# The token Fourier transform of a hybrid trunk on sums and differences of mirrored tokens, with half of the frequencies

## The reference, cut to what matters

```python
def _fourier(f, w_f):
    B, L, _ = f.shape
    fg = f.reshape(B, L, FNET_GROUPS, FNET_GROUP_DIM).astype(jnp.float32)
    z = jnp.fft.fft2(fg, axes=(1, 3), norm='ortho').real.astype(f.dtype)
    return z.reshape(B, L, FNET_DIM) @ w_f
```

## Time and profile before

| | |
|---|---|
| time, median of 3 runs | 1360.46 us (1359.41 to 1366.07) |
| profiled execution, its own time | 1359.2 us |
| its span, first to last instruction | 1357.4 us |
| mean granted TensorE clock | 0.966 |
| TensorE, VectorE, ScalarE, POOL busy | 91%, 69%, 46%, 23% |

### The profile page before, as it was taken

The page is one execution under the profiler, slowest core; times in us unless marked ns, Lnnn a source line. Parts: engine busy times, 40 slices in busy tenths (PEclk is TensorE's granted clock), DMA queues, the critical chain, the costliest instruction groups (busy, mean ns, idle before and its releaser), DMA issues.

```text
span 1357.4 us, 18907 instructions
## 1 busy us (share of the span) xinstructions
PE 1241.9 (91%) x7350; PEld 991.9 (73%) x7350; DVE 939.8 (69%) x1078; ACT 621.3 (46%) x688; POOL 311.4 (23%) x209
## 2 busy tenths in 40 slices
PE   2799979999999999999799269999999999999995
PEld 1588858997888999999799246666666666666663
DVE  1569866465666342712664869999999999999996
ACT  2421122223433222413112347777777777777774
POOL 2031010000333212323122502222222222222214
PEclk9899989999999989999899679999999999999998
DMA  9764661322110111224222999999999999999994
GB/s 293 251 191 148 213 148 36 105 94 70 47 48 20 44 63 62 63 94 177 103 65 109 350 317 356 381 382 383 382 382 381 381 383 382 383 382 382 383 316 174
DMA packets 156264, 302.89 MB, mean 223 GB/s; under 512 B 7058, under 2 KB 60821, under 8 KB 155952
## 3 DMA queue, kind: packets, MB, share of 16 engines
q1 hardware_dynamic: 145708, 272.87, 56.0%
q0 software_dynamic: 3872, 12.78, 4.3%
q10 hardware_dynamic: 6628, 16.44, 3.3%
HBM read 286.98 MB, written 15.08 MB: 223 GB/s over the span
## 4 chain that ended last, share of the span: by engine, by line
PE 84%; DVE 8%; ACT 2%; DMA 2%; issue 1%; POOL 1%; SPq 1%; ACTq 0%; POOLq 0%; DVEq 0%
PE bank L1466 16%; PE bank L1467 16%; PE bank L1468 16%; PE bank L1489 5%; PE bank L1494 4%; PE bank L1491 4%; PE bank L1490 4%; PE bank L1493 4%; PE bank L1492 4%; PE bank L1695 2%; DVE fa L1035 1%; PE bank L1668 1%; PE bank L1521 1%; DMA mask<-const_mask 1%; DMA g2r<-scratch_mods 1%
## 5 line engine op out<-in xcount | busy, mean ns | idle before, releaser
L869 ACT CAST h2r_a<-w_a 128x2048 fp32r<-128x2048 f32 x96 | 183.7, 1914 | 78.7 <-PE bank L1468 76.5
L1466 PE MATMUL bank<-h2r_a,xTh 128*80 128x512 f32 x384 | 152.3, 397 | 1.0 <-DVE xTl L1385 1.0
L1468 PE MATMUL bank<-h2r_a,xTl 128*80 128x512 f32 x384 | 150.3, 391 | 0.0
L550 POOL TENSOR_TENSOR half<-half 1x1 f32<-1x1 f32 x33 | 67.8, 2056 | 350.8 <-DVE ye L1433 347.9
L482 POOL TENSOR_TENSOR lring<-wring,hring 128x2048 fp32r<-128x2048 f32 x21 | 98.4, 4685 | 206.5 <-ACT hring L618 206.5
L1467 PE MATMUL bank<-l2r_b,xTh 128*80 128x512 f32 x320 | 125.7, 393 | 0.0
L1379 DVE TENSOR_TENSOR l2r_b<-w_a,h2r_b 128x2048 fp32r<-128x2048 f32 x48 | 110.3, 2299 | 17.8 <-ACT h2r_b L869 17.8
L1379 DVE TENSOR_TENSOR l2r_a<-w_a,h2r_a 128x2048 fp32r<-128x2048 f32 x48 | 109.6, 2283 | 12.0 <-ACT h2r_a L869 7.5
L1379 DVE TENSOR_TENSOR l2r_b<-w_a,h2r_a 128x2048 fp32r<-128x2048 f32 x48 | 109.9, 2289 | 10.1 <-ACT h2r_a L869 10.1
L1035 DVE SCALAR_TENSOR_TENSOR fa<-fa,cwT 128x655 f32<-128x655 f32 x120 | 111.7, 974 | 1.4
L1489 PE MATMUL bank<-hTh,hring 128*128 128x320 f32 x320 | 106.4, 332 | 4.8 <-DVE hTl L1097 3.6
(11 more groups left out here) (332 smaller groups left out, 3105.5 us busy)
## 6 DMA issues: line engine op xcount, KB each, us to landing
w_a<-in_w_e_gate SPq DMA_DIRECT2D x64, 1024.0 KB, 11.7
w_a<-in_w_e_up SPq DMA_DIRECT2D x64, 1024.0 KB, 12.4
w_b<-in_w_e_down SPq DMA_DIRECT2D x48, 1024.0 KB, 11.8
wring<-in_w_in SPq DMA_DIRECT2D x21, 1024.0 KB, 5.3
w_a<-in_w_e_down SPq DMA_DIRECT2D x16, 1024.0 KB, 12.7
fa<-in_w_ada SPq DMA_DIRECT2D x13, 1024.0 KB, 7.1
wring<-in_w_ada SPq DMA_DIRECT2D x11, 1024.0 KB, 5.6
wring<-in_w_out SPq DMA_DIRECT2D x4, 1024.0 KB, 5.2
```

The source lines that it names most:

```text
L869: act.copy(h2r[k % 3], w2[k]).then_inc(e_hi, 1)
L1466: pe.matmul(out, lh, rh, start=start, stop=False)
L1468: return pe.matmul(out, ll, rh, start=False, stop=stop)
```

## The change

The 512 latent tokens are folded: for tokens t = 1 to 255, e(t) = f(t) + f(512 - t) and o(t) = f(t) - f(512 - t); tokens 0 and 256 stay. In detail:

- After each f block ScalarE copies the latent tokens to a new buffer fs, VectorE makes sum, difference and a copy of two columns in eo (a new semaphore each way), ScalarE casts the high half from eo and VectorE the low half of 512 columns. f blocks carry 4 taps each (16 instead of 20).
- uv(g) is two jobs: 256 columns for the context tokens and 2 x 128 for the sums with the cosine table; then 2 x 128 for the differences with the sine table and one row for token 256.
- z(g): 260 columns of frequencies with 2 blocks of sums and one row; 256 columns with 2 blocks of differences; the context tokens as before. ScalarE copies the context result, one column and the sine part (to qs); VectorE then makes fold_back(g): the first half of the frequencies by a sum, the second half, written backwards, by a difference. z is now freed by VectorE.
- The two tables are cut to 1292 columns in one unit, loaded by three DMAs; with a unit less, the slots of all later units change.
- qs lies on the rows of the modulation stores, so ScalarE's wait for all sixteen stores moves ahead of the first uv cast.
- The uv loop has no taps; in 9 has none, and in 4, 5, 6, 7, 20 and 21 have 11 each. fold_back(3) stands behind the low half of in 9.
- The final stage uses the semaphores s_xt in place of s_fin.

```diff
+UNITS += [("ada", 18), ("ada", 19), ("dft", 0)] + [("ada", i) for i in range(20, 24)]
...
+HALF = NS // 2
+DFT_C, DFT_S, DFT_M = 0, 2 * (HALF + 4), 2 * (HALF + 4) + 2 * HALF
+DFT_N = DFT_M + HALF + 4
...
+BY_DVE = ("f", "uv", "z", "fnet", "na", "conv", "out")
...
+        fs = fa[:, 4608:5632].rearrange("p (b t) -> p b t", b=2)
+        eo = fa[:, 5632:6656].rearrange("p (b t) -> p b t", b=2)
+        qs = fa[:, SM + 512:SM + 1024].rearrange("p (b t) -> p b t", b=2)
...
+        H_SLOT = {u: n % 3 if n < 7 else 1 if n == 7 else 3 if n == 8 else (n + 1) % 2 for n, u in enumerate(SPLITS)}
...
+                if UNITS[u][0] == "dft":
+                    x, n = raw(u), HALF + 4
+                    tab = consts["dft_l"]
+                    sp.dma_start(x[:, DFT_C:DFT_S].rearrange("p (c k) -> p c k", c=2), tab[0, :, 0:2, 0:n]).then_inc(s_w[SLOT[u]], 16)
+                    sp.dma_start(x[:, DFT_S:DFT_M].rearrange("p (c k) -> p c k", c=2),
+                                 tab[1, :, 0:2, 0:HALF]).then_inc(s_w[SLOT[u]], 16)
+                    sp.dma_start(x[0:1, DFT_M:DFT_N], tab[0, 0:1, 2, 0:n]).then_inc(s_w[SLOT[u]], 16)
+                    return
...
@@ ScalarE
...
+                (_, b0), (_, b1) = job_halves(n)
+                act.copy(bh[:, i, 0:NP], b0[:, 0:NP])
+                if i >= 2:
+                    act.wait_ge(s_eo, i - 1)
+                act.copy(fs[:, i % 2, 0:TH - NP], b0[:, NP:TH])
+                act.copy(fs[:, i % 2, TH - NP:NS], b1).then_inc(s_fh, 1)
+                act.wait_ge(s_eo, i + 1)
+                act.copy(bh[:, i, NP:T], eo[:, i % 2, :]).then_inc(s_fh, 1)
                 if i >= 1:
                     mod_store(5 + 2 * i)
                 mod_store(6 + 2 * i)
-                if i in (1, 2):
-                    hi(U_OF[("dft", i - 1)])
+                if i == 1:
+                    hi(U_OF[("dft", 0)])
...
             def uv_hi(g):
-                for t in range(TT):
-                    n = J_OF[("uv", g, t)]
-                    act.wait_ge(s_job, n + 1)
-                    act.copy(uvh[:, g % 2, t, :], bank[n % 2][:, 0:256]).then_inc(s_uvh, 1)
+                w, n = g % 2, J_OF[("uv", g, 0)]
+                act.wait_ge(s_job, n + 1)
+                act.copy(uvh[:, w, 0:512], bank[n % 2][:, :]).then_inc(s_uvh, 1)
+                n += 1
+                act.wait_ge(s_job, n + 1)
+                act.copy(uvh[:, w, 512:768], bank[n % 2][:, 0:256])
+                act.copy(uvh[0:1, w, 768:896], bank[n % 2][0:1, 256:384]).then_inc(s_uvh, 1)
 
             act.wait_ge(s_rpb2, 16)
+            for st in s_mst:
+                act.wait_ge(st, 16 * 4)
             uv_hi(0)
             for g in range(4):
                 if g < 3:
                     uv_hi(g + 1)
                 n = J_OF[("z", g)]
                 act.wait_ge(s_job, n + 1)
-                bs, bp = job_bank(n)
-                act.copy(Z[:, g, NP:T], bs)
-                act.copy(Z[:, g, 0:NP], bp).then_inc(s_ja, 1)
+                zp, zq = bank[n % 2], bank[2 + n % 2]
+                act.copy(Z[:, g, 0:NP], zq[:, 0:NP])
+                act.copy(Z[:, g, NP + HALF:NP + HALF + 1], zp[:, HALF:HALF + 1])
+                if g >= 2:
+                    act.wait_ge(s_jd, freed(J_OF[("z", g - 2)])[1])
+                act.copy(qs[:, g % 2, :], zq[:, NP:NP + HALF]).then_inc(s_zq, 1)
 
             hi(U_OF[("in", 9)])
-            for st in s_mst:
-                act.wait_ge(st, 16 * 4)
...
@@ VectorE
...
+                dve.wait_ge(s_fh, 2 * i + 1)
+                x, y, w = fs[:, i % 2, :], eo[:, i % 2, :], i % 2
+                dve.tensor_tensor(y[:, 1:HALF], x[:, 1:HALF], x[:, NS - 1:HALF:-1], ALU.add)
+                dve.tensor_tensor(y[:, HALF + 1:NS], x[:, 1:HALF], x[:, NS - 1:HALF:-1], ALU.subtract)
+                dve.tensor_copy(y[:, 0:NS:HALF], x[:, 0:NS:HALF]).then_inc(s_eo, 1)
+                dve.tensor_tensor(bl[:, i, 0:NP], bank[n % 2][:, 0:NP], bh[:, i, 0:NP].bitcast(F32), ALU.subtract).then_inc(s_jd, 1)
                 rows_out(16 + 2 * i)
                 ada_mod(15 + 2 * i)
                 rows_out(17 + 2 * i)
                 ada_mod(16 + 2 * i)
-                if i in (1, 2):
-                    lo(U_OF[("dft", i - 1)])
-                conv(4 if i in (1, 2) else 6)
+                if i == 1:
+                    lo(U_OF[("dft", 0)])
+                dve.wait_ge(s_fh, 2 * i + 2)
+                dve.tensor_tensor(bl[:, i, NP:T], y, bh[:, i, NP:T].bitcast(F32), ALU.subtract).then_inc(s_fl, 1)
+                conv(4)
             ada_mod(23)
             lo(U_OF[("in", 8)])
 
             def uv_lo(g):
-                for t in range(TT):
-                    n = J_OF[("uv", g, t)]
-                    dve.wait_ge(s_uvh, TT * g + t + 1)
-                    dve.tensor_tensor(uvl[:, g % 2, t, :], bank[n % 2][:, 0:256], uvh[:, g % 2, t, :].bitcast(F32),
-                                      ALU.subtract).then_inc(s_jd, 1)
+                w, n = g % 2, J_OF[("uv", g, 0)]
+                dve.wait_ge(s_uvh, 2 * g + 1)
+                dve.tensor_tensor(uvl[:, w, 0:512], bank[n % 2][:, :], uvh[:, w, 0:512].bitcast(F32), ALU.subtract).then_inc(s_jd, 1)
+                n += 1
+                dve.wait_ge(s_uvh, 2 * g + 2)
+                dve.tensor_tensor(uvl[0:1, w, 768:896], bank[n % 2][0:1, 256:384], uvh[0:1, w, 768:896].bitcast(F32), ALU.subtract)
+                dve.tensor_tensor(uvl[:, w, 512:768], bank[n % 2][:, 0:256], uvh[:, w, 512:768].bitcast(F32),
+                                  ALU.subtract).then_inc(s_jd, 1)
+
+            def fold_back(g):
+                n = J_OF[("z", g)]
+                dve.wait_ge(s_zq, g + 1)
+                zp, q = bank[n % 2], qs[:, g % 2, :]
+                dve.tensor_tensor(Z[:, g, NP:NP + HALF], zp[:, 0:HALF], q, ALU.add)
+                dve.tensor_tensor(Z[:, g, T - 1:NP + HALF:-1], zp[:, 1:HALF], q[:, 1:HALF], ALU.subtract).then_inc(s_jd, 1)
 
             uv_lo(0)
             for g in range(1, 4):
                 uv_lo(g)
-                conv(6)
-
-            for i in (9, 4, 5, 6, 7, 20, 21):
+                fold_back(g - 1)
+            lo(U_OF[("in", 9)])
+            fold_back(3)
+            for i in (4, 5, 6, 7, 20, 21):
                 lo(U_OF[("in", i)])
-                conv(7)
+                conv(11)
...
@@ TensorE
...
+                w, n = g % 2, J_OF[("uv", g, 0)]
+                x = slice(0, P)
+                pe.wait_ge(s_fl, g + 1)
+                bank_free(n)
+                mm3(bank[n % 2][:, 0:256], bh[:, g, 0:P], bl[:, g, 0:P], gtab_h[:, 0:256], gtab_l[:, 0:256], True, True)
+                for j in range(2):
+                    x = slice(NP + j * P, NP + (j + 1) * P)
+                    last = mm3(bank[n % 2][:, 256 + j * P:256 + (j + 1) * P], bh[:, g, x], bl[:, g, x], gtab_h[:, 0:P], gtab_l[:, 0:P],
+                               True, True)
+                last.then_inc(s_job, 1)
+                n += 1
+                bank_free(n)
+                m = slice(NP + HALF, NP + HALF + 1)
+                mm3(bank[n % 2][0:1, 256:384], bh[:, g, m], bl[:, g, m], gtab_h[:, 0:P], gtab_l[:, 0:P], True, True)
+                for j in range(2):
+                    x = slice(NP + HALF + j * P, NP + HALF + (j + 1) * P)
+                    last = mm3(bank[n % 2][:, j * P:(j + 1) * P], bh[:, g, x], bl[:, g, x], gtab_h[:, P:2 * P], gtab_l[:, P:2 * P],
+                               True, True)
+                last.then_inc(s_job, 1)
+
             pe.wait_ge(s_cast, 4)
             uv(0)
             u = U_OF[("dft", 0)]
-            (ch, cl), (sh, sl) = slot(u), slot(u + 1)
+            th, tl = split(u)
+
+            def table(x, start, j, n):
+
+                return x[:, start + j * n:start + (j + 1) * n]
+
             for g in range(4):
                 if g < 3:
                     uv(g + 1)
                 if g == 0:
-                    lo_ready(pe, u + 1)
+                    lo_ready(pe, u)
                 n = J_OF[("z", g)]
-                pe.wait_ge(s_jd, freed(J_OF[("uv", g, TT - 1)])[1])
+                pe.wait_ge(s_jd, freed(J_OF[("uv", g, 1)])[1])
                 bank_free(n)
-                bs, bp = job_bank(n)
-                w = g % 2
-                for c in range(4):
-                    mm3(bs, uvh[:, w, c + 1, 0:P], uvl[:, w, c + 1, 0:P], ch[:, c, :], cl[:, c, :], c == 0, False)
-                    mm3(bs, uvh[:, w, c + 1, P:2 * P], uvl[:, w, c + 1, P:2 * P], sh[:, c, :], sl[:, c, :], False, c == 3)
-                mm3(bp, uvh[:, w, 0, 0:P], uvl[:, w, 0, 0:P], gtab_h[:, 0:P], gtab_l[:, 0:P], True, False)
-                mm3(bp, uvh[:, w, 0, P:2 * P], uvl[:, w, 0, P:2 * P], gtab_h[:, 2 * P:3 * P], gtab_l[:, 2 * P:3 * P],
+                w, kn = g % 2, HALF + 4
+                zp, zq, vh, vl = bank[n % 2][:, 0:kn], bank[2 + n % 2], uvh[:, w, :], uvl[:, w, :]
+                for j in range(2):
+                    x = slice(256 + j * P, 256 + (j + 1) * P)
```

(17 more changed lines are left out.)

47 lines of the change are left out of this document (15 added, 32 removed).

## The result

The changed kernel takes 1371.31 us in the median (1366.5 to 1376.7), the kernel before, on the same chip and interleaved, 1365.77 (1359.02 to 1368.79). The ratio is 1.0045, with a 95% interval of 1.0028 to 1.0063: slower by 5 to 6 us, where 1363.5 had been forecast and 1369.5 was the upper end of the range. One of the sixteen executions of the changed kernel, in the slow state (1461.0 us at a mean clock of 0.821), counts in the median, which is 1370.4 without it, but neither in the range nor in the ratio.

A forecast was written before the change was run, and what follows sets the result against it. TensorE was taken as nearly always busy outside Fourier-stage waits and hand-overs and attention's start. Fourier gain -7.5, clock +1.9, taps +7.3, attention clock +2.0 gave +3.7 on 1359.2, 1362.9, put at 1363.5 between two bases; range 1353 to 1369.5.

The forecast's parts named there:

- f blocks: The four f blocks ahead of the Fourier stage: extra copies and sums cost +0.5 us from first to fourth.
- Restart of TensorE: Fourier stage: last modulation store lands with the Bt loads' end, about 191.1; TensorE restarts at 192.6 instead of 181.95.
- Rival A: Fourier stage: last store doesn't wait for Bt loads, TensorE restarts 7.5 to 8.5 us earlier; 1355 us; chance 0.15.
- z(0) and the loop: Fourier stage: z(0) 3.9 us at half clock, then full-clock periods of 5.15 for 10.34; v jobs start 10.4 us earlier.
- rival B: Fourier loop doesn't return to full clock: period 6.6 us, 4.4 us more in all, 1368 us; chance 0.15.
- The v jobs: End of Fourier stage: second v job waits 3 us for fold_back(3), leaving 7.5 us of the gain.
- The clock drop behind it: After the gap behind the first v job: 3.8 us of work at half speed, +1.9 us, bounds 0 and 3.5.
- The taps: Ahead of attention: eleven taps instead of two behind in 21's low half, all nine extra exposed, +7.3 us.
- Half clock at attention: Start of attention: after about 8 us idle TensorE resumes at half clock for 3.8 to 4 us, +2.0 us.
- Sum: Whole kernel: -7.5 + 1.9 + 7.3 + 2.0 = +3.7 us on the profiled 1359.2, so 1362.9, put at 1363.5.
- the far half of B: The half of rival B's outcomes farther from the forecast, left out of the range 1353 to 1369.5.

The follow-up runs named there:

- the Bt-free run: Changed kernel with POOL issuing the eight attention-bias (Bt) loads only after the first uv cast: 1366.73 us, ratio 1.0013 to the kernel before.
- the run with 56 matmuls: Changed kernel plus 56 unused matmuls of 512 columns between uv(0) and uv(1), keeping TensorE busy through the wait: 1364.51 us, ratio 0.9994.
- the best version: Changed kernel, qs on idle columns, fold_back(3) before in 9's low half, in 8 split behind uv(1), no taps in fourth f block or before attention: 1346.62, 1342.05 us.

## Why the prediction was wrong

**f blocks**: +0.55 us for 0.5. Right.

**Restart of TensorE**: of the old stand of 6 us, three taps took 2.50 (176.52 to 179.03 in the chain of before), which the forecast's account of it left out. The forecast has the first cast at 191.1, which is 193.8 with the 2.7 us by which this execution was late; it was 191.93. That the last store is held up by the Bt loads was right, the Bt-free run shows it. That it goes last, behind all of them, was not. Packets by queue in the changed kernel, 190 to 191 and 191 to 192:

```profile
q0 software_dynamic: 45, 0.14, 92.8%
q1 hardware_dynamic: 33, 0.03, 22.0%
q10 hardware_dynamic: 2, 0.00, 0.2%
...
q0 software_dynamic: 43, 0.14, 86.1%
q1 hardware_dynamic: 25, 0.02, 16.4%
```

The three stores have twelve packets: none passes from 182 to 186, three in 186 to 188, seven in 188 to 190 and the last two in 190 to 191. After them q0 moves on at the same rate and runs dry only at 195. Rival A did not happen, as the wait is 9.76 us long where A has 1 to 2. The Trainium skill (DMA: Bandwidth & Descriptors, Queues, rings and completion order) has the engines serve queues by turns. The counts of q0 and q1 here agree (163 to 129 packets in 188 to 192); a last store that is issued by 182.1 and lands at 191.9 doesn't.

**z(0) and the loop, the step that failed**: that the clock is back when z(0) ends. Forecast: 3.9 us for z(0) at half clock, then full clock, periods of 5.15, and the v jobs 16.6 us after the start of z(0). Measured: 5.13, half clock until 221, periods of 8.75, and 26.15 (197.04 to 223.19). The difference is 9.55 us. It has two parts: the clock, 7.1 us, and the prices of the matmuls, 2.4.

The larger is rival B, to which I had given 0.15. Its point of decision was well put: the clock isn't back by the end of z(0), and it stays away. My argument against it, that the old loop holds 1.00 at a busy share of 2.96 of 4 us, is about another loop, at full clock. This one, of short matmuls, lost the clock in every profile, also where it was entered at full clock: for 3 us in the run with 56 matmuls, for 7 and for 31 in the two profiles of the best version. And it is slow to get it back. From TensorE's restart, or the fall of the clock if that came later, half clock lasted 28 us in the changed kernel, 19 to 35 in the five other versions with a stand of over 4 us and no filler (19 where the fold order alone was changed, 33 to 35 in the rest), and 7 to 10 in the three profiles of the old loop. What the run with 56 matmuls shows is that without the stand of 13 us the loop of the changed kernel is 7.0 us shorter; it doesn't show that the loop keeps its clock whenever it enters with it. TensorE isn't short of work at half clock: in the second profile of the best version it is busy 29.24 of 30 us at a mean of 0.53. The Trainium skill (TensorE: Matmul & The Clock Gate, A second HAM failure mode) ties low clock to idle spells between groups. The fall in the 56-matmul run fits that, since stretches busy only 1.64, 1.52 and 1.35 of 2 us come before it. The loop of the changed kernel has no idle spell from 193.39 to 226 and is at half clock for the first 28 us of it, and nothing in these runs says why. The old loop, which does pause at half clock (in the kernel before 0.3 us at each hand-over), had it back after 7 to 10. The reason stays open.

The smaller part, and with it the price of rival B, is the short matmuls. I had 6.6 us for a period at half clock; it is 8.75. "I double what the columns cost" went wrong with the short matmuls. At full clock 128 columns cost 0.11 and 256 cost 0.12: so 0.11 isn't the price of columns, but of what comes with every matmul that has new weights of 128 x 128. It doubles too. I had 0.107 for 128 columns at half clock; they take 0.213. The uv matmuls for token 256, with the same 128 columns and weights of a single column, do stand 0.107 apart at half clock (195.34 to 195.66 in the changed kernel's trace) and 0.06 at full clock in the run with 56 matmuls, which points to the weights. With six of them in z and twelve in uv that is 1.9 us a period. The four long steps around the one-row matmuls add 0.57 in z. With the gap for VectorE's fold gone (TensorE never waits), 6.6 - 0.4 + 1.9 + 0.6 = 8.7. At full clock these four steps cost 0.20 to 0.23 instead of 0.12, z is 2.87 instead of 2.4, the period 5.53 instead of 5.15. So even on the branch that I forecast the loop would have been 2.4 us longer: 1.2 at full clock, and 1.2 in z(0), which is at half clock on either branch.

With the measured prices, rival B is not 4.4 us above the forecast but 9.5: 1362.9 + 1.2 (z(0)) + 2 x 3.6 + 1.1 = 1372.4. That the profile stands near it (1373.6) is in part chance. 4.9 us of it aren't the change's, and without them it has 1359.2 + 9.4 = 1368.6, as the last store landed 1.9 us earlier than forecast and the 1.9 us behind the first v job did not come.

**The v jobs**: gap 2.56 us for 3. The clock drop behind it, +1.9, wasn't there in the changed kernel (clock 1.00 from 222 on) and was in the run with the 56 matmuls, whose gap is the same. A gap of 2.6 us can go either way.

**The taps**: +7.3, measured +7.31, and once more +7.30 in the kernel before. Half clock at attention: +2.0, measured +1.58 and +1.76.

**Sum**: the terms that were right are +0.55, +7.3 and +1.6. In the place of -8.0 stands 0: the shorter work and the fewer hand-overs pay for the wait (about 7 us of the stage) and the clock (another 7), and nothing is left. The range ended at 1369.5 because it was to leave out the far half of B; the likely mechanism had the wrong side of B, and B was priced 5 us too low. The base adds to it: on the median of sixteen executions the same terms would have given some 1369. That would have come near the result by luck, since they hold 8 us of gain in the stage that never came.

**Open**: the sixteen executions of before fall in two groups, around 1359 and 1366 us, and the profiled one (1359.2) is like the lower. Which stretch makes the difference isn't shown; the stretch ahead of the first f block, which is up to 8.6 us longer in one profile than in another, is one that could. Nor is it shown why the medians are 5.5 us apart where the changed work in the two profiles is 9.4 apart.

## What to carry to other kernels

When a change replaces long matmuls by short ones, price them from the start times of short ones, at both clocks: from 128 to 256 columns the price here hardly changes, since it is that of new weights, and it doubles at half clock. Ask of every stage in what state TensorE enters it, and whether its own loop keeps that state: a saving in a stage of short matmuls that is entered after a long stand may be paid out at half clock for its whole length. Moving unrelated work out of the way (the wait for a store, the order of the last fold, a few taps) turned a loss of 0.45% into a gain of 1.0%, and with the split of in 8 moved too it was 1.1 and 1.8% in two measurements. And take the base of a forecast from enough executions: three of them stood 5.3 us below sixteen. And filler that is moved out of a loop, like the taps, has to be counted to its last slot; the one just ahead of a dependent stage costs its full length and then the clock.

## What the runs showed of the hardware

- Half clock with TensorE busy throughout lasts very differently: 19 us in one execution and 28 in another, of kernels that are the same up to there, and 7 and 31 us in two executions of one kernel.
- Matmuls of 128 columns with new weights of 128 x 128 stand 0.11 us apart at full clock and 0.213 at half clock, of 256 columns 0.12 and 0.213; of 128 columns with weights of one column 0.06 and 0.107. The step onto a matmul with one row, the step off it and the step after each of these take 0.20 to 0.23 at full clock and 0.34 to 0.38 at half clock.
- Three stores of four packets each, issued behind eight loads of 192 KB on another queue, had landed some 10 us after the last was issued in four kernels (waits of 9.76, 9.34, 9.31 and 10.29 us) and within 1.35 us of the wait's start without them.
- VectorE's sum and difference with a reversed operand take 0.43 and 0.42 us for 255 columns (174.78 and 175.12 in the changed kernel's trace), and the write in reverse 0.41 (228.37), the same as a forward one of 256 (228.03, 0.42).
